# Expert stages written out without a loop, their first weights split ahead of routing, tokens' parts by half, overflow in quarters

## The reference, cut to what matters

```python
def grouped_moe_2(h, router_w, router_b, w_gate, w_up, w_down):      # layers e and o; 0 and 1 differ in the router
    aff = jax.nn.sigmoid((xf @ router_w).astype(jnp.float32))        # T x 16
    biased = (aff + router_b).reshape(T, N_GROUPS, EXPERTS_PER_GROUP_2)   # 4 groups of 4 experts
    grp_score = jnp.sum(lax.top_k(biased, TOP_K)[0], axis=-1)
    g_sel = jnp.argmax(grp_score, axis=-1)                           # one group for each token
    local = lax.top_k(biased[tok, g_sel], TOP_K)[1]                  # two experts in it
    w = aff[tok[:, None], expert]; w = w / jnp.sum(w, axis=-1, keepdims=True)
    ...
    hid = jax.nn.silu(xb @ w_gate[e]) * (xb @ w_up[e])               # 1024 -> 512
    return hid @ w_down[e]                                           # 512 -> 1024, times w, summed over the two

def rmsnorm(x, g):
    y = xf * lax.rsqrt(jnp.mean(xf * xf, axis=-1, keepdims=True) + NORM_EPS)
```

## Time and profile before

| | |
|---|---|
| median of 3 runs | 2485.01 us (2484.23 to 2486.5) |
| the profiled execution | 2484.54 us, its span 2482.6 us, 26176 instructions |
| TensorE busy (matmul) | 2168.1 us, 87% |
| VectorE, ScalarE, GpSimd busy | 1540.5, 1114.1, 89.2 us |
| DMA | 596.18 MB, 240 GB/s over the span |

### The profile page before, as it was taken

One profiled execution on the slowest core, in us unless ns is written; L12 is line 12 of the kernel. 1 busy time (PEld: TensorE's weight loads), 2 busy tenths in 40 slices (PEclk: granted clock), 3 DMA queues, 4 the chain that ended last, 5 costly groups with the idle time before them and its releaser, 6 DMA issues.

```text
span 2482.6 us, 26176 instructions
## 1 busy us (share of the span) xinstructions
PE 2168.1 (87%) x9572; PEld 1642.3 (66%) x9572; DVE 1540.5 (62%) x1956; ACT 1114.1 (45%) x1188; POOL 89.2 (4%) x82
## 2 busy tenths in 40 slices
PE   8899799899799969989969877989978687799996
PEld 4657478788465747878857646778743374677775
DVE  2743488778464348878752736878840353587886
ACT  1201176676110117767633516767720131576773
POOL 0110000000111000000010000000000000000000
PEclk9999799999999979999989987999989898799998
DMA  9665388788665518878835015879866222388883
GB/s 408 271 223 214 102 308 327 297 329 334 266 251 225 215 55 317 330 299 328 334 137 186 1 68 183 334 296 340 312 261 251 87 102 76 141 335 327 301 317 119
DMA packets 48682, 596.18 MB, mean 240 GB/s; under 512 B 5200, under 2 KB 7248, under 8 KB 8784
## 3 DMA queue, kind: packets, MB, share of 16 engines
q1 hardware_dynamic: 34560, 500.19, 53.5%
q0 software_dynamic: 8352, 59.77, 6.0%
q10 hardware_dynamic: 5680, 35.00, 3.9%
HBM read 591.79 MB, written 3.15 MB: 240 GB/s over the span
## 4 chain that ended last, share of the span: by engine, by line
PE 64%; issue 21%; DVE 7%; ACT 3%; DMA 3%; POOL 1%; DVEq 0%; ACTq 0%; POOLq 0%
PE bank L701 58%; PE bank L731 2%; PE bank L946 2%; DMA hi_ring<-in_ada 1%; POOL small L2264 1%; DMA x<-in_x_in 1%; PE bank L957 1%; DVE ring_parts L1595 1%; DVE work L1595 1%; ACT hi_ring_parts L1224 1%; ACT work L1224 1%; ACT mix L1224 1%; DVE mix L1684 0%; DVE hi_ring L1954 0%; DVE work_parts L1595 0%
## 5 line engine op out<-in xcount | busy, mean ns | idle before, releaser
L1595 DVE TENSOR_TENSOR ring_parts<-ring,hi_ring_parts 128x2048 fp32r<-128x2048 f32 x398 | 892.0, 2285 | 150.4 <-ACT hi_ring_parts L1224 150.2
L1224 ACT ACTIVATE hi_ring_parts<-ring 128x2048 fp32r<-128x2048 f32 x398 | 749.2, 1913 | 146.0 <-PE bank L701 115.4
L701 PE MATMUL bank<-hi_ring_parts,xT_parts 128*128 128x512 f32 x1024 | 340.6, 405 | 48.5 <-DVE ring_parts L1595 48.5
L1224 ACT ACTIVATE work<-bank 128x512 f32<-128x512 f32 (+6 forms) x215 | 113.1, 529 | 545.0 <-PE bank L701 426.8
L701 PE MATMUL bank<-hi_ring_parts,oT_parts 128*128 128x512 f32 (+1 forms) x1088 | 351.0, 389 | 4.6 <-DVE ring_parts L1595 4.6
L701 PE MATMUL bank<-hi_ring_parts,work_parts 128*128 128x512 f32 x1024 | 328.4, 392 | 24.9 <-DVE work_parts L1595 24.9
L701 PEld LDWEIGHTS bank<-hi_ring_parts,xT_parts 128*128 128x128 f32 x1024 | 199.1, 194 | 94.6 <-DVE ring_parts L1595 52.7
L701 PEld LDWEIGHTS bank<-hi_ring_parts,work_parts 128*128 128x128 f32 x1024 | 192.2, 188 | 70.2 <-issue 30.8
L701 PEld LDWEIGHTS bank<-hi_ring_parts,oT_parts 128*128 128x128 f32 x1088 | 204.4, 188 | 48.6 <-DVE ring_parts L1595 8.6
L701 PE MATMUL bank<-ring_parts,oT_parts 128*128 128x512 f32 (+1 forms) x576 | 219.2, 381 | 0.0
L701 PE MATMUL bank<-ring_parts,xT_parts 128*128 128x512 f32 x512 | 204.9, 400 | 0.0
(11 more groups left out here) (203 smaller groups left out, 2337.7 us busy)
## 6 DMA issues: line engine op xcount, KB each, us to landing
ring<-in_weights SPq DMA_DIRECT2D x238, 2048.0 KB, 7.9
hi_ring<-in_ada POOLq DMA_DIRECT2D x48, 1024.0 KB, 11.1
hi_ring<-in_weights ACTq DMA_DIRECT2D x12, 2048.0 KB, 7.7
work<-in_vecs POOLq DMA_DIRECT2D x8, 1024.0 KB, 5.1
bias_rows<-work ACTq DMA_DIRECT2D x8, 256.0 KB, 3.9
work<-bias_rows ACTq DMA_DIRECT2D x2, 1024.0 KB, 7.7
params<-in_prm ACTq DMA_DIRECT2D x1, 1389.5 KB, 13.0
consts<-in_cst ACTq DMA_DIRECT2D x1, 1040.0 KB, 18.7
```

Of the source, the lines that this page charges most:

```text
L701: ins = nc.tensor.matmul(o, lhsT, rhs, start=start, stop=stop)
L1224: return nc.scalar.activation(o, i, f, **kw)
L1595: return v.tensor_tensor(o, a, b, op)
```

## The change

1. `moe_jobs`, `experts` and the waits are written out for four groups in a row on TensorE, ScalarE and VectorE; the loop and its counts by register go. The former end of a round becomes a boundary like the others.
2. The first piece of weights of a stage is split by `split_expert` ahead of routing.
3. The tokens' high and low parts are made by half (four chunks each), with a wait for each half ahead of the gate product's halves.
4. The scaling or memset of the sum moves behind the first tokens' parts, the ada bias ahead of the routing.
5. The overflow section is written like a group: split parts, weights in quarters of 128 x 1024 (512 KB), loaded four ahead into eight places in `hi_ring`'s space, high parts in four places elsewhere, and a scatter of parts.
6. `rstd(n)` takes the root of the n columns in use: 2 by default, 8 twice in each of layers 0 and 1, and 4 in one place of layer o.

The diff, cut to its core:

```diff
-                with pe.Fori(0, BODIES) as it:
...
+                for g in range(GROUPS):
+                    for e in range(PER_GROUP):
+                        k = PER_GROUP * g + e
+                        if e == 0:
+                            for half in range(2):
+                                pe.wait_ge(xlo_ready, 2 * (GATHERS * layer + g) + half + 1)
+                                gate_up("g", k, (half,))
+                            if g:
+                                scatter(g - 1)
+                            gate_up("u", k)
+                        if e < PER_GROUP - 1:
+                            gate_up("g", k + 1, (0,))
+                            turn_hidden(k)
+                            gate_up("g", k + 1, (1,))
+                        else:
+                            gather_b(g + 1, 1)
+                            turn_hidden(k)
+                        down(k)
+                        if e == 0:
+                            gather_a(g + 1)
+                        if e < PER_GROUP - 1:
+                            gate_up("u", k + 1)
+                scatter(GROUPS - 1)
```

TensorE's overflow section (`wide` and `narrow` add three products for each chunk, `single` is a product without a release):

```diff
+                    wide("g", 0, range(4))
                     for e in range(PER_GROUP):
...
+                        wide("u", e, range(4))
+                        if e < PER_GROUP - 1:
+                            wide("g", e + 1, range(2))
+                        pe.wait_ge(ov_hidden, PER_GROUP * layer + e + 1)
                         for j in range(HC):
...
+                        ins.then_inc(ov_turned, 1)
+                        if e < PER_GROUP - 1:
+                            wide("g", e + 1, range(2, 4))
+                        narrow(e)
+                    for k, (T, n) in enumerate(OUTS):
+                        pe.wait_ge(ov_y_lo, 2 * layer + n + 1)
+                        for y, first, last in zip(y_parts(tag), (True, False), (False, True)):
+                            ins = single(psum[k][:, :], place_parts[0][:, T * P:(T + 1) * P], y[:, n * 512:(n + 1) * 512],
+                                         start=first, stop=last)
```

ScalarE:

```diff
+            def split_expert(tag, j):
+                for h in range(2):
+                    part = Half(tag, j, h)
+                    act.wait_ge(slot_full[part.slot], part.full)
+                    if part.free:
+                        act.wait_ge(halves_done, part.free)
+                    fn(part.hi, part.raw, ACT.Identity).then_inc(hi_ready, 1)
...
-                def gather_b(n, it=None):
-                    gather(n, 1, it)
-                    for half in range(2):
-                        banks.wait_drained(act, f"{tag}.xg{n}.{half}", it)
-                    fn(xg_hi[n % 2], xg[n % 2], ACT.Identity).then_inc(xhi_ready, 1)
+                def high(n, half):
+                    banks.wait_drained(act, f"{tag}.xg{n}.{half}")
+                    c = slice(4 * half, 4 * half + 4)
+                    fn(xg_hi[n % 2][:, c, :], xg[n % 2][:, c, :], ACT.Identity).then_inc(xhi_ready, 1)
+                def gather_a(n):
+                    whole(place_parts[n % 2], f"{tag}.at{n}")
+                    whole(slot_gate[:, n % 2, :], f"{tag}.sg{n}")
+                    gather(n, 0)
+                    high(n, 0)
+                def gather_b(n):
+                    gather(n, 1)
+                    high(n, 1)
...
+                    def split(what, e, parts=range(4)):
+                        for q in parts:
+                            i = 4 * POS[what, e] + q
+                            w = Quarter(tag, i)
+                            if w.free:
+                                act.wait_ge(ov_used, w.free)
+                            if i + HI_RING < QUARTERS:
+                                load(i + HI_RING)
+                            act.wait_ge(w.loaded, w.full)
+                            fn(w.hi, w.raw, ACT.Identity).then_inc(ov_hi, 1)
+                    for i in range(HI_RING):
+                        load(i)
+                    split("g", 0)
                     for e in range(PER_GROUP):
+                        split("u", e)
+                        act.wait_ge(ov_used, used(tag, "g", e))
+                        fn(esig[:, e % 2, :], psum[e % 2][:, :], ACT.Silu).then_inc(ov_sig, 1)
...
                         if e < PER_GROUP - 1:
+                            split("g", e + 1)
+                        split("d", e, range(2))
+                        act.wait_ge(ov_turned, PER_GROUP * layer + e + 1)
+                        fn(ehT[:, e % 2, :, :], psum[4][:, :].rearrange("p (c n) -> p c n", c=HC), ACT.Identity) \
+                            .then_inc(ov_hid_hi, 1)
+                        split("d", e, range(2, 4))
...
+                act.wait_ge(ada_summed, ADA_COLS * (l + 1))
+                split_expert(f"{tg}.moe", 0)
                 turned(f"{tg}.turn2")
...
+            split_expert("e.moe", 0)
             modulated("e.turn1", 0, 24)
```

VectorE and GpSimd:

```diff
                 slots(0)
                 overflow_control(layer)
                 low_tokens(0)
...
+                if tag[0] in "01":
+                    step(v.tensor_scalar(total, x[:, :, :], ALPHA, None, ALU.mult))
+                else:
+                    step(v.memset(total, 0.0))
...
                 turned(f"{tg}.turn2")
+                modulation_bias(l)
+                split_expert(f"{tg}.moe", 0)
                 route(tg, "b_router", True)
-                step(v.tensor_scalar(mix[:, :, :], x[:, :, :], ALPHA, None, ALU.mult))
-                modulation_bias(l)
...
             adaptive_norm("e.turn1", 0, pr("norm_ffn")[:, 0:8], 32, 24)
+            split_expert("e.moe", 0)
             route("e", "router_b_2", False)
-            step(v.memset(ysum("e.moe"), 0.0))
...
-            def rstd():
+            def rstd(n=2):
                 stats[0] += 1
                 pool.wait_ge(var_ready, stats[0])
-                nc.gpsimd.tensor_tensor(stat_out, stat_in, cs("half"), ALU.pow).then_inc(rstd_ready, 1)
+                nc.gpsimd.tensor_tensor(stat_out[:, 0:n], stat_in[:, 0:n], cs("half")[:, 0:n], ALU.pow) \
+                    .then_inc(rstd_ready, 1)
```

More of the change, by code:

```diff
@@ L354, in program @@
         PLACE = [5760, EX + 3712]
-        ov_place = cut(work, 5504, NT * P)
         place_parts = [cut(work_parts, at, NT * P) for at in PLACE]
@@ L646, in program @@
         YACC = 4096
-        def yacc(tag):
-            return cut(work, YACC, D)
         def y_parts(tag):
@@ L1943, in _ @@
+                    dve.sem_inc(ov_done, 1)
+                dve.wait_ge(ov_done, layer + 1)
             adas = [0]
```

668 lines of the change are left out of this document (318 added, 350 removed).

## The result

| | before | after |
|---|---|---|
| median | 2484.62 us (2482.39 to 2486.5) | 2374.12 us (2371.58 to 2376.35) |
| profiled execution, span | 2484.54, 2482.6 us | 2373.05, 2371.1 us |
| TensorE busy | 2168.1 us | 2135.7 us |

The ratio is 0.9555, 95% interval 0.9539 to 0.9572: 110.5 us less, where 102.5 were forecast (2382, inside the range of 2360 to 2412).

The account below looks back on a forecast made before the run. Inside the groups TensorE's own stream was taken as the bound, so only its waits could go. Gains of 39.6 + 26.5 - 5 + 29.4 + 12 = 102.5 us took 2484.5 to 2382, range 2360 to 2412.

Parts of the forecast that it names:

- B: Seam in the middle of each expert stage, where the loop starts over: written out, 6.6 us gained in each, 26.5 in all.
- the clock: Starts of the four expert stages: without idle time the first products run at full speed, 2.0 us each, 8 gained.
- up weights' low part: Starts of the four expert stages: the low half of the up weights comes late, 1.2 us each, charged at -5.
- C: Tokens by half inside the groups: 0.6 us more on ScalarE, partly returned in e and o; -5, ends -8 and 0.
- A: Starts of the four expert stages: first gate product follows the gather, with weights split ahead of routing; 39.6 us gained together.
- E: GpSimd's roots taken over fewer than 16 columns: 12 us gained, between 0 if all cost is fixed and 22.
- D: Overflow section in layer e, rewritten with quarters loaded four ahead and ScalarE last at 1.6 us a quarter: 29.5 us gained.
- second rival: Roots cost the same and the clock falls at the stage starts as before: 12 + 8 less gain, 2402 us; 14%.
- fifth rival: The moved weight splits aren't hidden by the logits: 4.6 us in each of four layers, 2400 us; 8%.
- first rival: Overflow paced slower than forecast, by loads or TensorE at 1.2 GHz: 2.3 us a quarter, 34 more, 2416 us; 10%.
- the third: Overflow: every quarter's load waits for the one before, 4.0 us each, 2489.5 us, slower than before; 3%.
- fourth rival: Straight code is fetched too late: 26 more instruction packets as a bound, 34 us, 2416 us; 5%.

Follow-up runs that it names:

- split_behind: Changed kernel with the first weights' split of each expert stage put back behind the tokens' parts on ScalarE and VectorE: 2407.74 us.
- seam_back: Changed kernel, still straight code, but the second group is scattered and summed before the third group's gate product in each stage: 2405.75 us.
- tokens_whole: Changed kernel with the tokens' high and low parts made for all eight chunks in one operation each: 2390.36 us.
- ov_half_bytes: Changed kernel with each overflow quarter loading half its bytes, operations of the same sizes, output not the reference's: 2375.64 us.
- ov_serial: Changed kernel with each overflow quarter loaded only when ScalarE is ready for it, nothing ahead: 2495.95 us.
- roots16: Changed kernel with every root on GpSimd taken over 16 columns again: 2395.57 us.
- ov_ahead1: Changed kernel with the overflow's quarters loaded one ahead in place of four: 2419.8 us.
- down_early: Changed kernel with each group's last expert starting its down product on products needing only the hidden values' high part: 2378.42 us.

## Why the prediction came out as it did

The direction and the four kinds of places were right, and so were the mechanisms but one: the overflow section is paced by TensorE and not by ScalarE. The terms, set beside the stretches:

| terms of the prediction | forecast | measured |
|---|---|---|
| inside the stages: B 26.5, the clock 8, up weights' low part -5, C -5 | 24.5 | 26.4 |
| starts and between: A's 30.8 + 7.0 - 1.2, E 12 | 48.6 | 51.4 |
| overflow, D | 29.5 | 33.7 |
| sum | 102.6 | 111.5 |

That the second row fits within 3 us is partly luck: E was 9.5 too low in it and A 6.7 too high.

**A.** The first gate product at the gather's end at a high clock: shown in 0 and 1 (0.36, 0.29). In e and o it comes 1.6 to 1.7 after the gather, so the sign "within 1 us in all four layers" failed there: the first half's copies now end 0.2 behind the gather. It comes 1.5 after the copies' end; before it was 9.4 after them, so 7.9 of the 8.1 came. The idle time that went is 28.3 in all, not 30.8. That it also cost the clock is shown by split_behind, with 8.6 against the 8 forecast, so the second rival falls on that half. The up weights' low part waited as forecast, 1.24 us, but in e and o alone. The split stayed hidden behind the logits; VectorE still idled 2.42, 0.67, 1.33 and 2.75 there (layers 0, 1, e, o), no less than the 0.4 to 0.8 I had left, so the fifth rival falls. ScalarE's moved split delayed the logits of layer 0 by 1.4, not 1.2.

**B.** 26.5 against 27.8 by seam_back. In the kernel before, TensorE's products in the stages take 13.7 us more than after; split_behind puts 8.6 of these at the starts, so 5.1 are left for the seams, and with 19.4 of idle time B is 24.5 by that reading. The ring kept up without its pause, at share 0.89.

**C.** Mis-sized: -5, where tokens_whole shows -3.2. That the 0.6 on ScalarE counts in full in e and o was right (1.44 against 0.76 to 0.78 at eight places, 5.4 where 4.8 were forecast), and so is what comes back there (3.1 against 2.4, at the six boundaries). What was wrong is layers 0 and 1, which lost 0.8 and not 2.4. The up weights' low part, which I had at -5, cost 2.5, as it waited in two layers alone.

**D.** Mis-sized, 29.5 against 33.7. The step that failed is "ScalarE 1.06, 0.34 and about 0.2 for address registers and waits, 1.6": the trace has 1.36, and that is TensorE's six products. The costs don't add up on ScalarE, because its queue does the register work and the issue while the copy before is still running: where only landings hold it, its period is 1.25 to 1.30, so its own is no more than that. (The expectation of ov_half_bytes still took 1.36 for ScalarE's own.) From the first high part (1775.75, 5.7 after the last down product, where 5.8 was forecast) to the end of the last it takes 72.5 us and not 80; the pace alone would give 11.5 less, and some 4 went into waits, 2.85 of them for the last expert's turn. The tail to the last sum is 12.8 and not 9.6: TensorE waits 2.21 us for the last hidden values, and in the 5.3 us behind that its clock is 0.50. "ScalarE the fullest engine" was wrong: TensorE is. The bound of 38 was that case. The first rival (slower pace) falls; the third needs loads without depth, and ov_serial shows its price was right.

The Trainium skill (DMA: Bandwidth & Descriptors, Bandwidth, Measured) would have transfers of 1 MiB or more. With four loads of 512 KB ahead the stretches above have up to 398 GB/s, and ov_half_bytes with 256 KB was no slower, so the rule speaks against nothing here. The Trainium skill's fit (DMA: Bandwidth & Descriptors, Anatomy of one DMA — SWDGE (gpsimd) path), made for loads that GpSimd issues, gives an estimated 3.2 us for such a load alone; the row of one that GpSimd issues and ov_serial's, which ScalarE issues, both have 4.0. So the prediction's "the row here agrees on the latency" was wrong, and the measurement decides.

**E.** Mis-sized, 12 against 21.5 (roots16). "Near the middle" was no argument. Between all columns and all fixed, the rows give 0.94 us for 2, 1.66 for 8 and 3.08 for 16, so about 0.7 fixed and 0.15 a column, and a root of two waits 2.1 less. VectorE's waits for roots are 23.4 us less in the trace after.

**The rest.** With E at 21.5, 29.9 of the second row are left for A, against 36.6. Of the 6.7 missing, 2.5 is idle time that stayed and 0.2 the turned x; the remaining 4.0 is no more than the scatter shown below, and stays open. The fourth rival (instructions fetched too late) falls: 23 packets more were fetched, near its bound, with no time lost that the trace shows.

## What to carry to other kernels

Put the preparation of a stage's first operand ahead of the chain of small operations that precedes it, and count the clock with the idle time, since at the starts both went and came back together here. When TensorE waits for VectorE, look one engine further back: the wait was ended by VectorE, but moving VectorE's work gained nothing, while ScalarE's splits, moved ahead of its own waits on top of it, gained 33 us (2369.8 to 2336.3). The stream of small loads needed depth and not size here: one, two and four loads of 512 KB in flight gave 4.2, 2.5 and 1.5 us a quarter in the mean, the last no longer set by the loads. When an engine keeps step with another, look for the places where it waits for something else: only these showed how fast ScalarE could go.

## What the hardware showed that was not expected

ScalarE's queue issues a DMA 0.13 us after its current operation has begun (1807.38 and 1807.51 above), so a load written behind a copy does not wait for it. With a wait for TensorE written ahead of the load it came 0.98 us after (1801.30 and 1802.28).

A 512 KB load took 4.0 us from issue to landing alone, 4.7 with a second in flight (the median of ov_ahead1) and 5.8 with four.

The clock after a stage's end is not the same in two executions of the same code. From the end of layer 1 to the start of layer e the changed kernel took 257.69 us, down_early 261.58, seam_back 261.51, ov_ahead1 257.59 and ov_half_bytes 261.7, with the same instructions there. The same 15.2 us, beginning 15.2 us after the layer's stage, the changed kernel first, then seam_back, are granted 0.68 and 0.52:

```profile
1219.30:1234.50 15.20, 8.12 (x37) 7.26 (x38) 10.85 (x19) 7.94 (x10) 2.75 (x2) 0.68 0.58 190
```

```profile
1234.20:1249.40 15.20, 8.21 (x28) 7.04 (x29) 10.85 (x18) 7.93 (x10) 2.74 (x2) 0.52 0.58 176
```

TensorE does the same work there at a different clock, and the stretch differs by some 4 us. The runs of one kernel lie up to 13.9 us apart (ov_half_bytes), so this is a part of the scatter, and the rest was not placed. Nor does idle time of one length always end in the same clock: seam_back's 3.54 us left 0.50 in three layers and 1.00 in layer 1.
